# Row factors of the first block from the feature-major copy of x, the residual rows loaded later, and the first transfers on two queues

## The reference, cut to what matters

```python
def rmsnorm(x, g):
    r = lax.rsqrt(jnp.mean(xf * xf, axis=-1, keepdims=True) + NORM_EPS)
    return (xf * r * g).astype(x.dtype)

h = jnp.concatenate([meta, x], axis=1)        # 16 meta tokens, then 256 tokens
hn = rmsnorm(h, pre_norm_g[layer])
proj = jnp.einsum('bld,dc->blc', hn, w_in[layer])   # 2048 -> 6656 columns
...                                           # two attention mixers, gates, w_out
h = h + rmsnorm(y, post_norm_g[layer])
```

## Time and profile before

| | us |
|---|---|
| Median of 3 runs (lowest to highest) | 1819.62 (1819.14 to 1824.45) |
| The profiled execution, its own time | 1823.38 |
| Its span in the trace | 1821.3 |
| PE busy | 1788.1 (98%) |
| DVE busy | 1105.9 (61%) |
| ACT busy | 813.5 (45%) |
| POOL busy | 157.3 (9%) |
| Mean granted clock of TensorE | 0.992 of full speed |

### The profile page before, as it was taken

One profiled execution on the slowest core, in us unless ns is written; L12 is line 12 of the kernel. 1 busy time (PEld: TensorE's weight loads), 2 busy tenths in 40 slices (PEclk: granted clock), 3 DMA queues, 4 the chain that ended last, 5 costly groups with the idle time before them and its releaser, 6 DMA issues.

```text
span 1821.3 us, 24694 instructions
## 1 busy us (share of the span) xinstructions
PE 1788.1 (98%) x9943; PEld 1540.6 (85%) x9943; DVE 1105.9 (61%) x1316; ACT 813.5 (45%) x1135; POOL 157.3 (9%) x164
## 2 busy tenths in 40 slices
PE   7999999999999999999999999999999999999997
PEld 7999768888798788888888898888888888888886
DVE  4545755455566466567776556665665666666666
ACT  5334555544453544444444444344444444434443
POOL 0104465000000023000000000000000000000000
PEclk9999999999999999999999999999999999999998
DMA  9554433365486544565565556555555555555552
GB/s 323 186 174 139 139 116 130 125 207 187 139 256 190 156 139 139 162 185 182 188 185 186 186 184 208 190 194 189 189 184 184 186 194 186 193 186 184 185 186 91
DMA packets 253949, 324.67 MB, mean 178 GB/s; under 512 B 6048, under 2 KB 189984, under 8 KB 253344
## 3 DMA queue, kind: packets, MB, share of 16 engines
q1 hardware_dynamic: 251616, 320.31, 54.2%
q10 hardware_dynamic: 2256, 3.28, 0.5%
HBM read 321.47 MB, written 2.10 MB: 178 GB/s over the span
## 4 chain that ended last, share of the span: by engine, by line
issue 63%; PE 28%; POOL 5%; DMA 1%; ACT 1%; DVE 1%; SPq 0%; POOLq 0%; DVEq 0%
PE acc L528 4%; PE acc L488 4%; PE acc L490 4%; PE acc L489 4%; PE acc L529 2%; PE acc L516 2%; PE acc L517 2%; PE acc L515 2%; DMA raw<-w_in 1%; POOL ybuf L1983 1%; PE aux L650 1%; PE scores L616 1%; POOL tmp L1961 1%; POOL alibi L1974 1%; PE acc L502 0%
## 5 line engine op out<-in xcount | busy, mean ns | idle before, releaser
L1390 DVE TENSOR_TENSOR wlo<-raw,whi 128x1024 fp32r<-128x1024 f32 x591 | 736.0, 1246 | 590.0 <-ACT whi L1021 588.8
L1021 ACT ACTIVATE whi<-raw 128x1024 fp32r<-128x1024 f32 x591 | 625.5, 1060 | 763.8 <-PE acc L529 451.8
L528 PE MATMUL acc<-hboth,whi 128*128 128x512 f32 x2176 | 770.0, 399 | 0.0
L529 PE MATMUL acc<-hboth,wlo 128*128 128x256 f32 x2176 | 609.2, 280 | 0.0
L528 PEld LDWEIGHTS acc<-hboth,whi 128*128 128x128 f32 x2176 | 408.7, 188 | 101.9 <-issue 3.3
L529 PEld LDWEIGHTS acc<-hboth,wlo 128*128 128x128 f32 x2176 | 410.5, 189 | 0.4
L488 PE MATMUL acc<-whi,fhi 128*128 128x512 f32 x352 | 137.2, 390 | 0.0
L490 PE MATMUL acc<-whi,flo 128*128 128x512 f32 x352 | 137.1, 389 | 0.0
L489 PE MATMUL acc<-wlo,fhi 128*128 128x512 f32 x352 | 137.0, 389 | 0.0
L515 PE MATMUL acc<-xboth,whi 128*128 128x272 f32 x320 | 93.4, 292 | 6.3 <-DVE wlo L1390 6.3
L516 PE MATMUL acc<-xboth,whi 128*128 128x272 f32 x320 | 93.3, 292 | 0.0
(11 more groups left out here) (258 smaller groups left out, 2352.4 us busy)
## 6 DMA issues: line engine op xcount, KB each, us to landing
raw<-w_in SPq DMA_DIRECT2D x115, 1024.0 KB, 5.5
raw<-w_gate_up SPq DMA_DIRECT2D x88, 1024.0 KB, 5.0
raw<-w_down SPq DMA_DIRECT2D x44, 1024.0 KB, 5.1
raw<-w_out SPq DMA_DIRECT2D x32, 1024.0 KB, 5.1
raw<-w_branch_a SPq DMA_DIRECT2D x8, 1024.0 KB, 5.7
raw<-w_branch_b SPq DMA_DIRECT2D x8, 1024.0 KB, 5.7
xres<-x SPq DMA_DIRECT2D x1, 2048.0 KB, 16.4
bias<-rel_rows ACTq DMA_DIRECT2D x2, 1024.0 KB, 8.3
```

The source lines that it names most:

```text
L528: nc.tensor.matmul(o.rearrange("p (s t) -> p s t", t=TOK), hi, both[:, :, kt, 0:TOK], start=kt == 0, stop=False)
L529: done = nc.tensor.matmul(o[:, 0:TOK], lo, both[:, 0, kt, 0:TOK], start=False, stop=kt == tiles - 1)
L1021: nc.scalar.activation(whi[:, j % 4], raw[:, j // 2, 2 * (j % 2):2 * (j % 2) + 2, :], ACT.Copy).then_inc(hi_ready, 1)
L1390: nc.vector.tensor_tensor(wlo[:, j % 4], raw[:, j // 2, 2 * (j % 2):2 * (j % 2) + 2, :], whi[:, j % 4].bitcast(F32), ALU.subtract).then_in ...
```

## The change

It does four things. (1) The squares and sums for the row factors are taken from `xt`: ACT squares `xt` in place in two halves after both halves of the activations are made, DVE sums over the eight feature tiles of each (`xsum`), and PE sums over the partitions with a matmul whose stationary side is -0.5 everywhere, so that each partition gets the whole row of sums. DVE turns that into variance plus epsilon in `rbc`, and POOL raises all of `rbc` (128 x 272) to the power -0.5. Two transposes in block 2 give the factors as columns for the evictions of later blocks. `metax` is gone. (2) `xres` is loaded after block 3's weights; block 1's weights come ahead of the identity and the tables. (3) The first transfers are split: `gcol` and the first two parts of `xt` are issued by ACT's queue, the first two feature tiles of weights are separate transfers, and each weight load now precedes its part of `xt`. PE starts with 11 matmuls on zeros. (4) The work on the lambda vectors and rope tables moves from block 1 to blocks 3 and 4.

```diff
+            def sum_squares():
+                bank = aux_bank()
+                minus_half = dims(half[:, 0:1], [0, P])
+                for k in range(2):
+                    pe.wait_ge(sums1, k + 1)
+                    nc.tensor.matmul(bank[:, 0:TOK], minus_half, xsum[:, k, :], start=k == 0, stop=k == 1)
+                pe.wait_ge(sums1, 3)
+                nc.tensor.matmul(bank[:, TOK:KEYS], minus_half, metasum[:], start=True, stop=True).then_inc(aux_ready, 1)
+                aux_used("sumsq", (var1, 1))
+
+            def rows_of_r():
+                pe.wait_ge(rbc_ready, 1)
+                pe.wait_ge(ident_in, 16)
+                bank = aux_bank()
+                for i in range(TT):
+                    done = nc.tensor.transpose(bank[:, i * P:(i + 1) * P], rbc[:, i * P:(i + 1) * P], ident)
...
-            for _ in range(15):
+            for _ in range(11):
...
-                    if b == 1 and j == 1:
-                        pe.wait_ge(ident_in, 16)
-                        pe.wait_ge(rstd1, 1)
-                        broadcast_r(ss, "rbc", meta=True)
+                    if b == 1 and j == 2:
+                        sum_squares()
+                    if b == 2 and j == 2:
+                        rows_of_r()
...
-            x_part(0)
-            sp.dma_start(gcol, t["start_c"][:, P:P + 56]).then_inc(start_in, 16)
-            sp.dma_start(raw[:, 0, 0:2], first[0][:, 0:2]).then_inc(first_in, 16)
-            x_part(1)
+            for k in range(2):
+                sp.dma_start(raw[:, 0, k], first[0][:, k]).then_inc(first_in[k], 16)
             sp.dma_start(raw[:, 0, 2:4], first[0][:, 2:4]).then_inc(raw_in[0], 16)
             for u in range(1, 4):
+                sp.dma_start(raw[:, u], first[u]).then_inc(raw_in[u], 16)
                 x_part(u + 1)
-                sp.dma_start(raw[:, u], first[u]).then_inc(raw_in[u], 16)
             sp.dma_start(metat[:], t["meta_t"]).then_inc(metat_in, 16)
+            halved_block(1, w1, W1[1][2] * CW)
             sp.dma_start(ident, t["start_c"][:, 0:P]).then_inc(ident_in, 16)
-            sp.dma_start(xres[:], t["x"][0].rearrange("(i p) d -> p i d", p=P)).then_inc(xres_in, 16)
...
-            for q in range(1, Q_WOUT):
+            for q in range(2, Q_WOUT):
...
+                if q == 3:
+                    sp.dma_start(xres[:], t["x"][0].rearrange("(i p) d -> p i d", p=P)).then_inc(xres_in, 16)
...
+            act.dma_start(gcol, t["start_c"][:, P:P + 56]).then_inc(start_in, 16)
+            for c in range(2):
+                lo, hi = XT_PARTS[c]
+                act.dma_start(xt[:, lo:hi, :], t["x_t"][:, lo:hi, :]).then_inc(x_in[c], 16)
...
                     if b == 1 and j < 2:
-                        act.wait_ge(xres_in, 16)
-                        nc.scalar.activation((vb, qta)[j][:].rearrange("p a b -> p (a b)")[:, 0:D], xres[:, j, :], ACT.Square,
-                                             accum_out=ss[:, j:j + 1]).then_inc(squares1, 1)
-                    if b == 1 and j == 3:
-                        take("rbc", rbc[:], KEYS, rbc_ready)
+                        act.wait_ge(stat_ready, G_X + 4 + 4 * j)
+                        y = xt[:, 8 * j:8 * j + 8, :]
+                        nc.scalar.activation(y, y, ACT.Square).then_inc(squares1, 1)
+                    if b == 1 and j == 1:
+                        nc.scalar.activation(metasq[:], metat[:], ACT.Square).then_inc(squares1, 1)
...
                 if b == 1 and j == 3:
+                    dve.wait_ge(aux_ready, use["sumsq"])
+                    nc.vector.tensor_scalar(rbc[:], aux[(use["sumsq"] - 1) % 2][:, 0:KEYS], -2.0 / D, EPS, ALU.mult, ALU.add).then_inc(var1, 1)
                     dve.wait_ge(rbc_ready, 1)
                     take_turned(8, four_tiles(qtb, acc[0]), rbc[:, 0:TOK], SCALE_B)
...
+                    if b == 1 and j in (0, 1):
+                        dve.wait_ge(squares1, j + 1)
+                        nc.vector.reduce_sum(xsum[:, j, :], xt[:, 8 * j:8 * j + 8, :].rearrange("p k t -> p t k"), AX).then_inc(sums1, 1)
...
                     if j == 0:
                         pool.wait_ge(var1, 1)
-                        chain.after(chain.step(rsqrt(ss[:, 0:2])))
-                        rsqrt(ss[0:META, 2:3]).then_inc(rstd1, 1)
+                        nc.gpsimd.tensor_tensor(rbc[:], rbc[:], dims(half[:, 0:1], [0, KEYS]), ALU.pow).then_inc(rbc_ready, 1)
```

More of the change, by code:

```diff
@@ L223, in build @@
         xt = place("xt", [P, KT, TOK], at=o_ybuf)
-        metax = place("metax", [META, D], at=o_1 + 8192)
+        metasq = place("metasq", [P, KT, META], at=o_1 + 29184)
+        xsum = place("xsum", [P, 2, TOK], at=o_1 + 30208)
+        metasum = place("metasum", [P, META], at=o_1 + 32256)
         metat = place("metat", [P, KT, META], at=o_1 + 37376)
@@ L302, in build @@
         x_in = [sem(f"x_in{c}") for c in range(len(XT_PARTS))]
-        first_in, first_hi, first_lo = sem("first_in"), sem("first_hi"), sem("first_lo")
+        first_in, first_hi, first_lo = [sem(f"first_in{k}") for k in range(2)], sem("first_hi"), sem("first_lo")
         xres_in, metat_in = sem("xres_in"), sem("metat_in")
-        meta_in, start_in, ident_in, consts_in = sem("meta_in"), sem("start_in"), sem("ident_in"), sem("consts_in")
+        start_in, ident_in, consts_in = sem("start_in"), sem("ident_in"), sem("consts_in")
         lam_in, grow_in, poolw_in, gfin_in = sem("lam_in"), sem("grow_in"), sem("poolw_in"), sem("gfin_in")
@@ L308, in build @@
         out_done = sem("out_done")
-        squares1, var1, rstd1 = sem("squares1"), sem("var1"), sem("rstd1")
+        squares1, sums1, var1, rows_rstd = sem("squares1"), sem("sums1"), sem("var1"), sem("rows_rstd")
         rope_tables, zeroed, half_set, lam_sums, lam_exp, lam_ready = (
@@ L557, in back_to_rows, with broadcast_r @@
                 aux_used(("meta rows", n), (rows_taken, n + 1))
-            def broadcast_r(r, name, meta=False):
+            def sum_squares():
[13 more added lines that the diff above has]
+                    done = nc.tensor.transpose(bank[:, i * P:(i + 1) * P], rbc[:, i * P:(i + 1) * P], ident)
+                done.then_inc(aux_ready, 1)
+                aux_used("rows of r", (rows_rstd, 1))
+            def broadcast_r(r, name):
                 bank = aux_bank()
@@ L563, in broadcast_r @@
                     done = nc.tensor.matmul(bank[:, i * P:(i + 1) * P], dims(r[:, i:i + 1], [0, P]), ident, start=True, stop=True)
-                if meta:
-                    done = nc.tensor.matmul(bank[:, TOK:KEYS], dims(r[0:META, 2:3], [0, P]), ident[0:META, 0:META], start=True, stop=True)
                 done.then_inc(aux_ready, 1)
-                aux_used(name, (rbc_ready, {"rbc": 1, "rbc2": 2, "rbc3": 3}[name]))
+                aux_used(name, (rbc_ready, {"rbc2": 2, "rbc3": 3}[name]))
             def x_stat(kt, i):
@@ L1010, in split @@
                 if isinstance(g, int) and g == 0:
-                    act.wait_ge(first_in, 16)
+                    act.wait_ge(first_in[0], 16)
                     nc.scalar.activation(whi[:, 0, 0], raw[:, 0, 0], ACT.Copy).then_inc(first_hi, 1)
+                    act.wait_ge(first_in[1], 16)
                     nc.scalar.activation(whi[:, 0, 1], raw[:, 0, 1], ACT.Copy).then_inc(hi_ready, 1)
@@ L1094, in block1_side @@
                     if prev == 7:
-                        act.wait_ge(rstd1, 1)
+                        act.wait_ge(rows_rstd, 1)
                     what = W1[prev][0]
@@ L1181, in _ @@
                         meta_hi_part()
[L1182 to L1186, removed]
-                    if b == 1 and j < 2:
-                        act.wait_ge(xres_in, 16)
-                        nc.scalar.activation((vb, qta)[j][:].rearrange("p a b -> p (a b)")[:, 0:D], xres[:, j, :], ACT.Square,
-                                             accum_out=ss[:, j:j + 1]).then_inc(squares1, 1)
-                    if b == 1 and j == 3:
-                        take("rbc", rbc[:], KEYS, rbc_ready)
-                    if b == 2 and j == 0:
+                    if b == 1 and j < 2:
+                        act.wait_ge(stat_ready, G_X + 4 + 4 * j)
[3 more added lines that the diff above has]
+                        nc.scalar.activation(metasq[:], metat[:], ACT.Square).then_inc(squares1, 1)
+                    if b == 2 and j == 4:
+                        act.wait_ge(aux_ready, use["rows of r"])
+                        bank = aux[(use["rows of r"] - 1) % 2]
+                        nc.scalar.activation(ss[:, 0:2], dims(bank[:, 0:1], [P, 2]), ACT.Copy).then_inc(rows_rstd, 1)
+                    if b == 4 and j == 0:
                         act.wait_ge(lam_sums, 1)
@@ L1588, in _ @@
                     turned1(b, j)
-                    if b == 1 and j == 5:
+                    if b == 3 and j == 5:
                         dve.wait_ge(lam_in, 64)
@@ L1597, in _ @@
                         done.then_inc(lam_sums, 1)
-                    if b == 1 and j == 6:
```

(12 more changed lines are left out.)

## The result

The changed kernel took 1854.3 us (median of 4 runs, 1853.1 to 1858.2), the kernel before, run beside it, 1819.8 us. The ratio is 1.0189, with a 95% interval of 1.0177 to 1.0202: slower by 34.5 us, where 1855 was forecast. The profiled execution took 1854.8 us with a span of 1852.8.

The account below looks back on a forecast made before the run. PE's matmul stream, busy 98% of the span, was taken as the bound. Block 1's piece 4 moves from 55.9 to 89.2 + 1.9 + 0.6 = 91.7 us; 1819.6 + 35.8 = 1855.4, say 1855, range 1832 to 1862.

Parts of the forecast that it names:

- The power: POOL's power on 272 columns before block 1's piece 4: 0.57 us plus 0.16 for each further column, 43.9 us.
- its other end: Low end for POOL's power on 272 columns: 0.98 us, what simpler work on 272 columns costs.
- The path to it and from it: Block 1: sums reach DVE at 41.9, power starts at 42.4, hand-offs, `qtb` and `wlo` follow, piece 4 at 89.2 us.
- The hole before block 1: PE's 6.32 us wait before block 1's first matmul vanishes with earlier weight loads; block 1 starts at 34.5 us.
- The step that failed: Block 0's piece 2 starts at 17.3 us, between 15.0 and 17.8, as the third part of `xt` now comes last.
- piece 2 of block 0 at or before 16 us: Sign of a wrong forecast: such a start would say the swap of loads costs nothing.
- The squares and sums: ACT squares 1.89 us each, DVE sums 2.4 each, done before 36 us; PE asks at 40.7, margin some 5.
- The restart: After PE's 41 us idle in block 1, slow-clock steps cost 1.9 us, as after the earlier hole.
- The transposes: Two added transposes in block 2 cost PE 2 x 0.28 = 0.6 us, from 4.5 us for 16.
- The sum: Piece 4 of block 1 at 91.7 us with restart and transposes, against 55.9 before: slower by 35.8 us.
- The first rival: POOL's power is short, costing what other work on 272 columns costs, so the kernel takes 1812.4 us; chance 0.13.
- the deciding point: POOL's power at 2.8 us: below that, PE's hole before block 1's piece 4 is gone and the kernel is faster.

Follow-up runs that it names:

- the product: Changed kernel with POOL's power on the 272 columns replaced by a multiply of the same operands, so row factors are left out: 1810.55 us, ratio 0.9953.
- the lab kernel: Changed kernel plus five DVE instructions behind the variance and four POOL powers behind the first, on data nobody reads, to time them: 1854.36 us.
- half of the columns: Changed kernel with POOL's power on 128 of 272 columns and a multiply on the other 144: 1832.68 us, ratio 1.0073.
- columns a second time: Unchanged repeat of the changed kernel with sums as columns, power on 128 x 2 and 16 x 1, then spread by PE: 1812.02 us, ratio 0.9949.
- the first two experiments: Changed kernel with POOL's power replaced by a multiply on all 272 columns (1810.55 us), then on 144 of them (1832.68 us).

## Why the prediction was right

- **The power.** This was the term that decided, and it held to 0.2 us: 43.9 forecast from the slope between one, two and four columns, 43.71 measured. The line through the rows of the operation itself was worth more than the rows of other operations at the right width. The product on the same tile took 0.64 us, where the forecast had 0.98 as its other end. The estimate from the Trainium skill's page GPSIMD Engine Reference, section 3.1 (Elementwise), was 0.6 to 0.8 us. The product's 0.64 agrees with that estimate, and for the power it would have been too low by a factor of some 60.
- **The path to it and from it.** The sums reached DVE at 41.77 (forecast 41.9), the power started at 42.36 (42.4), and piece 4 at 88.79 (89.2). PE's wait was 40.98 us, forecast 41.
- **The hole before block 1.** Gone, and block 1 started at 34.58, forecast 34.5. The loads back in their old place bring a hole back, of 4.6 us.
- **The step that failed, and another that hid it.** Piece 2 was put at 17.3 us, because the bytes ahead of the third part of `xt` were the same. It came at 16.04: the last of what ACT waits for lands at 11.97, where the weights came at 13.63 before. By the prediction's own test, "piece 2 of block 0 at or before 16 us" (met but for 0.04 us), the changed places of the two loads cost next to nothing. The 1.3 us won there were lost again by 20 us: 16 steps took 0.21 instead of 0.12 us, 1.5 us. The prediction had put the 11 zero matmuls off the path, which they are as a wait, but it said nothing of the clock. That block 1 started at the forecast time is thus two errors that cancel, and luck besides: the lab kernel, the same program up to there, began block 1 at 33.41, and in the profiles of the kernels with the product, with half of the columns and with columns a second time it began at 32.97 to 33.26, each time with a slow stretch that lay earlier.
- **The squares and sums.** Mis-sized: 3.9 us each instead of 2.4, because they were costed by a sum of 1024 elements from another place. PE asked at 40.7 and they were done at 38.8, so the margin was 1.9 us and not 5. It held; with late loads it did not.
- **The restart.** 1.4 us instead of 1.9: 13 slow steps, not 18.
- **The transposes.** 0.6 us for two came from a group read as 16 transposes; its 32 rows are 32 transposes, so the group gives 0.28 for two. In the trace the steps around the two are 0.2 us longer. Matmuls in fp32 do leave two rows each (two of them are the `x4` on line 567), so the price of the sums was read rightly.
- **The sum.** Up to piece 4 the profiles give 88.8 + 1.4 + 0.6 - 55.9 = 34.9 us, forecast 35.8, and the runs 34.5. With 0.2 for the transposes and 55.73, where piece 4 really starts in the trace of before, it is 34.7.
- **The first rival** put a kernel with a short power at 1812.4 and the deciding point at 2.8 us. With the product the kernel took 1810.6, which is 1.8 us less, and in its profile block 1 started 1.5 us earlier than forecast. The waits of the first two experiments give 2.7.

What stays open: why the slow stretch in block 0 comes. By its steps of 0.21 us it is in all seven profiles with 11 zero matmuls (at 8 to 14 us in five of them, at 17 to 20 in two), and in none of the three with 15. PE had been idle for 1.5 to 2.6 us before its first real matmul in the seven, and for 1.2 us at most in the three; which of this decides is not shown. In three of the five early ones, those of the product, of half the columns and of the lab, the granted clock reads 1.00 all the while, so the steps have to be looked at too. It costs at most 1.5 us. Where it lay early, the wait before piece 2 took up most of it: with all loads early, block 1 then began at 33.0 to 33.4 us, and with 15 zero matmuls at 32.9 and 33.5; where it lay at 17 to 20 us, block 1 began at 34.6. Single runs of one kernel lie 2 to 6 us apart (before: 1818.3 to 1824.4 beside the experiments), so the runs can't price it.

## What to carry to other kernels

Price an instruction by rows of its own operation at other sizes, and extend the line; rows of other operations at the right size can be off by a factor of 45 (0.98 us for 43.7). Before an elementwise function goes onto the spread form of a value, ask whether it can be done on the narrow form first: two columns and a matmul that spreads them cost nothing here that the runs can tell, 272 columns cost 42 us. And take a change of several parts apart: here one part (the order of the loads, which the sums from `xt` made possible) carried a gain of 9 us, one (the wide power) lost 44 (1854.3 against 1810.6 with the product), and one (the first transfers) did nothing that can be measured.

## What the runs showed of the hardware

- The power on POOL costs 0.16 us for each further column of a tile, and is no cheaper on 16 partitions than on 128: 0.57, 0.73, 1.05, 1.64, 6.23, 10.5, 20.7 and 43.7 us for 1, 2, 4, 8, 32, 64, 128 and 272 columns, and 11.4 for 16 partitions by 64.
- A sum on DVE over 2048 values takes 3.87 us when neighbours are 1 KB apart (256 results) and 2.27 when they stand in a row (8 results).
- The same program can have its stretch of 1.2 GHz in different places of its first 20 us, in two executions on two chips (granted clock 0.50 at 18 to 20 us in one, at 8 to 10 in the other).
- The granted clock can read 1.00 while PE's steps are those of the slow clock (in the lab kernel 28 steps from 8.02 to 14.13 us).
